# Where the normed activation and its weights lie against each other in the on-chip memory: a ramp of 32, 48, 64 bytes in place of 0, 16, 32, 48, 64

## What is computed

```
h = _rmsnorm(x, norm_pre_w[l])
proj = jnp.einsum('bsd,de->bse', h, w_in[l])
(q, k, v, o_g, z_a, i_pre, f_pre, u_b, z_b, g_a, g_b) = _partition(proj)
...
br_a = jnp.einsum('bsc,cd->bsd', y_a, w_proj_mlstm[l])
br_b = jnp.einsum('bsc,cd->bsd', y_b, w_proj_pool[l])
merged = jax.nn.sigmoid(g_a) * br_a + jax.nn.sigmoid(g_b) * br_b
out = jnp.einsum('bsd,de->bse', merged, w_out[l])
x = x + _rmsnorm(out, norm_post_w[l])
```

## Time and profile before

| | us |
|---|---|
| median of 3 runs | 1459.64 (1459.16 to 1460.74) |
| the profiled execution | 1462.16 |
| its span, first to last instruction | 1460.5 |
| TensorE busy | 1435.6 (98%) |
| VectorE busy | 850.6 (58%) |
| ScalarE busy | 707.5 (48%) |
| granted TensorE clock, mean | 0.995 |

### The profile page before, as it was taken

One profiled execution on the slowest core, in us unless ns is written; L12 is line 12 of the kernel. 1 busy time (PEld: TensorE's weight loads), 2 busy tenths in 40 slices (PEclk: granted clock), 3 DMA queues, 4 the chain that ended last, 5 costly groups with the idle time before them and its releaser, 6 DMA issues.

```text
span 1460.5 us, 27819 instructions
## 1 busy us (share of the span) xinstructions
PE 1435.6 (98%) x10878; PEld 1370.6 (94%) x10878; DVE 850.6 (58%) x1054; ACT 707.5 (48%) x929; POOL 63.1 (4%) x95
## 2 busy tenths in 40 slices
PE   6999999999999999999999999999999999999997
PEld 6999998899999999999999999888999999999786
DVE  5676674546655666545454545556555545667754
ACT  5545544545555444434344444446433346667543
POOL 0000000001110000000000000001000002111000
PEclk8999999999999999999999999999999999999999
DMA  6655645655555555555655556656555553334553
GB/s 228 201 190 184 201 166 192 196 178 177 168 175 193 175 186 190 174 194 182 199 189 191 193 190 214 247 173 217 203 172 169 178 174 121 121 121 136 208 198 122
DMA packets 71940, 266.01 MB, mean 182 GB/s; under 512 B 8088, under 2 KB 8096, under 8 KB 70944
## 3 DMA queue, kind: packets, MB, share of 16 engines
q1 hardware_dynamic: 69840, 253.12, 51.9%
q0 software_dynamic: 1440, 10.63, 2.1%
q10 hardware_dynamic: 576, 1.05, 0.2%
HBM read 260.56 MB, written 4.20 MB: 181 GB/s over the span
## 4 chain that ended last, share of the span: by engine, by line
PE 93%; DVE 3%; ACT 1%; DVEq 1%; issue 1%; DMA 0%; ACTq 0%; POOL 0%; SPq 0%; POOLq 0%
PE ps L350 23%; PE ps L354 22%; PE ps L352 22%; PE ps L342 6%; PE ps L343 6%; PE ps L344 6%; PE ps L462 2%; DVE wl L1220 1%; DVEq L1215 1%; PE ps L748 1%; PE ps L540 1%; PE ps L551 1%; DMA xn<-in_x 0%; PE ps L589 0%; ACT wh L900 0%
## 5 line engine op out<-in xcount | busy, mean ns | idle before, releaser
L1220 DVE TENSOR_TENSOR wl<-raw,wh 128x1024 fp32r<-128x1024 f32 x474 | 580.0, 1227 | 501.1 <-ACT wh L900 492.6
L900 ACT ACTIVATE wh<-raw 128x1024 fp32r<-128x1024 f32 x474 | 499.9, 1060 | 555.9 <-PE ps L354 426.7
L350 PE MATMUL ps<-xh,wh 128*128 128x256 f32 x1792 | 499.7, 279 | 3.0 <-DVE xl L1229 1.8
L352 PE MATMUL ps<-xl,wh 128*128 128x256 f32 x1792 | 498.0, 278 | 0.0
L354 PE MATMUL ps<-xh,wl 128*128 128x256 f32 x1792 | 497.9, 278 | 0.0
L350 PEld LDWEIGHTS ps<-xh,wh 128*128 128x128 f32 x1792 | 337.9, 189 | 3.7 <-DVE xl L1229 2.2
L352 PEld LDWEIGHTS ps<-xl,wh 128*128 128x128 f32 x1792 | 338.1, 189 | 0.1
L354 PEld LDWEIGHTS ps<-xh,wl 128*128 128x128 f32 x1792 | 338.0, 189 | 0.0
L350 PE MATMUL ps<-x2h,wh 128*128 128x256 f32 (+1 forms) x688 | 199.2, 290 | 1.0 <-DVE avt L1387 0.4
L354 PE MATMUL ps<-x2h,wl 128*128 128x256 f32 (+1 forms) x688 | 194.8, 283 | 0.0
L352 PE MATMUL ps<-x2l,wh 128*128 128x256 f32 (+1 forms) x688 | 194.5, 283 | 0.0
(11 more groups left out here) (337 smaller groups left out, 1772.8 us busy)
## 6 DMA issues: line engine op xcount, KB each, us to landing
raw<-in_w_stream SPq DMA_DIRECT2D x474, 512.0 KB, 3.3
xn<-in_x SPq DMA_DIRECT2D x4, 512.0 KB, 7.7
xr<-in_x POOLq DMA_DIRECT2D x1, 2048.0 KB, 12.3
x_kept<-xr POOLq DMA_DIRECT2D x1, 2048.0 KB, 9.1
x1r<-x_kept POOLq DMA_DIRECT2D x1, 2048.0 KB, 10.0
mrow<-bound_rows POOLq DMA_DIRECT2D x8, 128.0 KB, 3.5
poolw<-in_pool_w POOLq DMA_DIRECT2D x1, 1024.0 KB, 6.3
postw<-in_post_w POOLq DMA_DIRECT2D x1, 1024.0 KB, 5.2
```

Source lines behind the costliest of these rows:

```text
L350: pe.matmul(out_at(j), whr[:, c, f], hi(kc)[:, tokens], start=st, stop=False, skip_group_check=True)
L352: pe.matmul(out_at(j), whr[:, c, f], lo(kc)[:, tokens], start=False, stop=False, skip_group_check=True)
L900: act.activation(slot_view(wh_at[r], layout), raw[r][:, :, :], ACT.Copy).then_inc(wh_done, 1)
L1220: tt(slot_view(wl_at[r], layout), raw[r][:, :, :], slot_view(wh_at[r], layout).bitcast(F32), ALU.subtract).then_inc(split_done, 1)
```

## The change

The activation's ramp is cut to 0, 16, 32, 32, ... bytes (`SHORT`), and the by-feature weights that go with it start 224 bytes (56 elements) into their slot. The place becomes -224, that is 32, then 48, then 64 for all chunks from the third on. For `v` the weights start 32 bytes in: -32, -16, 0, 0, .... The ramps of `yh` and `zh`, and the layouts of `pa` and `pb`, stay. The same instructions are issued in the same order on every engine; only start addresses differ. Two things follow from the borders: the first six chunks of the first `v` group stand at 32, 48, 64, 64, 64, 64, and the first six chunks of the first `wo` group, split in the layout of `ga`, at 32 in place of 0. The 48 small matmuls of the gates (L519 to L521) read the activation at its new addresses too.

```diff
 RAMP = [4 * min(kc, 4) for kc in range(KC + 1)]
+SHORT = [4 * min(kc, 2) for kc in range(KC + 1)]
 BY_FEATURE, BY_TOKEN, SECOND, SECOND_KEYS = (48, 512), (0, 512), (0, 528), (16, 528)
-ON_RAMP, TOKEN_RAMP = (0, 512), (16, 512)
-LAYOUT_OF = {"qk": ON_RAMP, "o": ON_RAMP, "z": ON_RAMP, "u": ON_RAMP, "zb": ON_RAMP, "ga": ON_RAMP, "gb": ON_RAMP, "pa": ON_RAMP, "pb": ON_RAMP,
-             "v": TOKEN_RAMP, "wo": BY_TOKEN, "uv": BY_TOKEN, "w2": BY_TOKEN, "cq": SECOND_KEYS, "ckv": SECOND_KEYS,
+ON_RAMP, ON_SHORT, TOKEN_SHORT = (0, 512), (56, 512), (8, 512)
+LAYOUT_OF = {"qk": ON_SHORT, "o": ON_SHORT, "z": ON_SHORT, "u": ON_SHORT, "zb": ON_SHORT, "ga": ON_SHORT, "gb": ON_SHORT, "pa": ON_RAMP, "pb": ON_RAMP,
+             "v": TOKEN_SHORT, "wo": BY_TOKEN, "uv": BY_TOKEN, "w2": BY_TOKEN, "cq": SECOND_KEYS, "ckv": SECOND_KEYS,
...
-    def ramped(t):
+    def ramped(t, at=RAMP):
 
-        return lambda kc: t[:, kc * S + RAMP[kc]:(kc + 1) * S + RAMP[kc]]
+        return lambda kc: t[:, kc * S + at[kc]:(kc + 1) * S + at[kc]]
...
-        X, Y, Z = (ramped(xh), ramped(xl)), (ramped(yh), ramped(yl)), (ramped(zh), ramped(zl))
+        X, Y, Z = (ramped(xh, SHORT), ramped(xl, SHORT)), (ramped(yh), ramped(yl)), (ramped(zh), ramped(zl))
...
-            high_parts(ramped(xh), b, "norm_pre", s_x_high)
+            high_parts(ramped(xh, SHORT), b, "norm_pre", s_x_high)
...
-            low_parts(ramped(xl), ramped(xh), b, "norm_pre", s_x_high, s_x_low)
+            low_parts(ramped(xl, SHORT), ramped(xh, SHORT), b, "norm_pre", s_x_high, s_x_low)
```

More of the change, by code:

```diff
@@ L518, in _ @@
             o = ps[0:GATE_W, 4, 0:S]
-            pe.matmul(o, wgh[:, kc, :], ramped(xh)(kc), start=kc == 0, stop=False)
-            pe.matmul(o, wgl[:, kc, :], ramped(xh)(kc), start=False, stop=False)
-            last = pe.matmul(o, wgh[:, kc, :], ramped(xl)(kc), start=False, stop=kc == KC - 1)
+            pe.matmul(o, wgh[:, kc, :], ramped(xh, SHORT)(kc), start=kc == 0, stop=False)
+            pe.matmul(o, wgl[:, kc, :], ramped(xh, SHORT)(kc), start=False, stop=False)
+            last = pe.matmul(o, wgh[:, kc, :], ramped(xl, SHORT)(kc), start=False, stop=kc == KC - 1)
         last.then_inc(s_gate_sums, 1)
```

## The result

| | before | changed |
|---|---|---|
| median, us | 1460.19 (4 runs, 1459.16 to 1460.89) | 1473.72 (4 runs, 1472.58 to 1475.36) |
| ratio | | 1.0088, 95% interval 1.0075 to 1.0101 |
| span of the profiled execution, us | 1460.5 | 1472.9 |

The kernel became slower by 0.9%. The prediction said 1455.7, with a range up to 1467.5: it was wrong. The time lies near the rival "the groups fall into the slow pace at 64", form (a), which gave 1475.9; the slow pace is indeed what came, but in 21 of the 27 groups and not in all.

A forecast was written before the change was run, and what follows sets the result against it. The prediction took TensorE's matmul start pace as the bound. By-feature groups 4.05 plus `v` 0.15 minus `wo` 0.23 saved 3.97 us, from 1459.64 to 1455.7; own range 1455.0 to 1456.8, wider range 1455.0 to 1467.5 (80%).

The forecast's parts named there:

- the groups fall into the slow pace at 64: Rival: by-feature groups entering at 32 keep 1.41 us a chunk, 0.60 us a slow group; chances 16%, 11%, 17% by form.
- form (a): All 27 by-feature groups slow: +16.2 us, 1475.9 with the `v` and `wo` terms; 17% for all or nearly all.
- What bounds the kernel: TensorE, busy 98% of the span: the pace at which matmuls start sets the time, neither weights nor evacuation.
- If place alone counts, the new group is the old one from its chunk 2 on.: By-feature groups: six chunks take 8.25 us instead of 8.40, 0.15 a group, 4.05 us over 27 groups.
- After a whole chunk at place 0 it doesn't matter how the group was entered: Old ramp: `z` groups, behind other matmuls, matched `qk`: chunks 1 to 3 took 4.25 against 4.24 us, chunk 4 1.36.
- The three forms: Slow groups: all 27, 1475.9 (17%); the 12 behind other matmuls, 1464.7 (16%); the 15 others, 1466.9 (11%).
- The prices: By-feature groups: a slow group costs 0.60 us net, a fast one saves 0.15 us.
- `v`: Second `v` group's six chunks take 8.22 us instead of 8.27: 0.05 a group, 0.15 us for three groups.
- `wo`: First six `wo` chunks, moved from place 0 to 32, take 1.40 instead of 1.36 us each: at most 0.23 us more.
- Splits' addresses, gate matmuls: Splits written at 224 bytes cost nothing, covered by ScalarE's and VectorE's waits; the 48 gate matmuls stay within 0.1 us.
- The first chunk pays for entering: Rival: new chunk 0 still costs about 1.44 us; 27 by-feature groups save only 2.6 us, giving 1457.1; 12%.
- Place counts for nothing: Rival: place has no effect on the matmuls' pace, time stays at 1459.6 us; 3%.

The follow-up runs named there:

- e10: Changed kernel, every address kept, first matmul of each by-feature group on the normed activation issued twice: 1471.43 us, one run.
- e2: Changed kernel with the weights at 0 and the activation at 32, 48, 64 (same places): 1477.97 us, ratio 1.0113 to the kernel before.
- e8: Kernel before, `gb` and `v` weights moved so `gb` stays at place 64 and the last three `v` groups at 0: 1463.66 us, ratio 1.0015.
- e1: Changed kernel with the full ramp 0, 16, 32, 48, 64 back, activation and weights both 32 bytes further: 1461.90 us, ratio 1.0006 to the kernel before.
- e3: Changed kernel with places 0, 32, 48, 64, the step at 16 left out, weights at 0: 1480.18 us, ratio 1.0129 to the kernel before.
- e6: Changed kernel with all 16 chunks of by-feature groups on the normed activation at place 112: 1487.07 us, ratio 1.0171 to the kernel before.
- e7: Changed kernel with places climbing 16, 32, 48, 64: 1476.07 us, ratio 1.0098 to the kernel before.
- e4: Changed kernel with no ramp, place 64 in every chunk, `v` at 0 throughout: 1471.82 us, ratio 1.0078 to the kernel before.
- e5: Changed kernel with by-feature groups on the normed activation held at place 192, `v` at 0: 1462.27 us, ratio 1.0005 to the kernel before.
- e9: Changed kernel, activation held 64 bytes in, different weight starts for the first two chunks of some groups, the rest at place 64: 1466.27 us, one run.
- e11: Changed kernel, activation held, by-feature groups at place 64, sixteen of them starting with two chunks at 0: 1456.73 us, ratio 0.9982 to the kernel before.
- e12: e11 with `pa` and `pb` also held at place 64 and no start at 0 for `ga` 2 to 4: 1453.76 us, ratio 0.9963 to the kernel before.

## Why the prediction was wrong, point by point

- **What bounds the kernel**: right. The difference lies in the pace of TensorE's matmuls; no wait took part.
- **The step that failed**: "If place alone counts, the new group is the old one from its chunk 2 on." Place alone doesn't count. The new chunk 0 has the old chunk 2's relative place but is entered otherwise, and 21 of 27 groups ended at 1.413 (e10: with a changed entry alone, 19 of the 27 change their pace; e2, e8: the pair of addresses takes part too). I had seen both paces at 64 in the earlier trace rows and named the danger, and still gave the forecast to the case in which nothing is carried in.
- **"After a whole chunk at place 0 it doesn't matter how the group was entered"**: right as far as e1 and e3 go, in each of which all 27 groups came out alike, and it meant that removing that chunk removed what made the result the same everywhere. But the chunk only makes it the same, not good: with 0, 32, 48, 64 all came out slow.
- **The three forms**: the split was none of them, so that form (a) comes within 2.2 us of the measured time is in part luck. Both kinds of entry gave both paces: of the groups behind other matmuls 11 of 12 were slow, of the 15 others 10. Nor does the pace of the group before decide: the second `qk`, behind a slow group, was fast, the third, behind a fast one, slow.
- **The prices**: right. 0.59 to 0.62 us for a slow group where the prediction had 0.60, and 0.13 to 0.14 saved in a fast one where it had 0.15. With 21 and 6 the prediction's own numbers give 21 x 0.60 - 6 x 0.15 - 0.15 + 0.23 = +11.8. The groups gave +12.4: 0.33 of it is `pb`'s, which I didn't have, and the rest are the hundredths in the prices.
- **`v`**: right, 0.05 a group. **`wo`**: right, 0.20 against 0.23; the first six chunks take 8.39 (910.34 to 918.73). In the kernel before they took 8.19:

```profile
898.21 0.40 PE L342 MATMUL ps<-wh,mh 128*128 128x512 f32 x1
...
906.40 0.39 PE L342 MATMUL ps<-wh,mh 128*128 128x512 f32 x1
```

- **`pb`, left out**: its addresses are untouched, but it is entered from `gb`, whose weights moved. Chunk 0 takes 1.41 (743.29 to 744.70) against 1.36 in the earlier trace rows, chunks 1 and 2 2.85 against 2.87, chunk 3 1.41 against 1.36: 0.08 a group. It was 0.06 in e1, e2, e3, e6, e7 and e8, 0.04 in e10, and nothing in e4, e5, e9 and e11, where `gb` had been fast with its weights at 0 or at 128. In e8 the last chunks of `gb` stand at the same addresses as before and only their pace is the slow one. That a neighbour pays for moved addresses or for a slow group ahead of it was not in the sum.
- **Splits' addresses, gate matmuls**: nothing, as said. ScalarE 707.2 against 707.5, VectorE 850.5 against 850.6.
- **"The first chunk pays for entering"**: wrong. The first chunk took 1.40 from the fourth `qk` group on, 1.41 in the third.
- **"Place counts for nothing"**, with the rule of the Trainium skill, page "SBUF — State Buffer", section "Who interferes with whom", by which TensorE has two independent read ports and waits on nobody: that place counts for nothing agrees with no run here. Held places gave 1.36, 1.41, 1.42 and 1.44 a chunk for the same matmuls (e4, e6). Whether it is the reads of the two operands that get in each other's way is not shown, and nothing here shows TensorE waiting for another engine's reads.

## What to carry to other kernels

When equal matmuls show two paces at the same addresses anywhere in the trace, suspect a state that is entered and kept, and look at what stands ahead of each group. A warm-up that looks like pure cost (here 0.24 us a group) may be what fixes the state, and its worth is the groups times the length behind it. Don't judge a place by a chunk that passes through it: hold it for a whole group, behind each kind of work that comes before it, before building on it, and profile more than one execution where the times scatter. The cheapest form found here was to hold both operands' addresses across groups, tiles and loop turns, and to spend two chunks at place 0 only where other matmuls break the sequence. That start was followed by the fast pace in all 34 groups that had it in the profiled executions of e9, e11 and e12; how often an execution falls out of it is not shown.

## What was not expected of the hardware

- The same matmuls at the same addresses run at 1.360 or at 1.413 us a chunk of twelve, and keep that for a group or for 191 chunks (e12); with one matmul more in each group's first chunk, 19 of the 27 groups changed sides, in both directions (e10).
- Moving both operands by the same 16 bytes from chunk to chunk is no cheaper than moving them against each other: 1.41 to 1.42 in `gb`, 1.37 to 1.39 in `v` (e8), where held addresses give 1.360.
- Two chunks with the weights 32 bytes in and two with them 16 bytes in, both under an activation at 64 (places 32 and 48), took the same 1.400 and 1.396 (e9), while a chunk at place 48 with the activation at 48 and the weights at 0 took 1.42.
- What it is that locks, and why place 0 leads to the fast pace and 0, 32, 48 to the slow one, no run here shows; that stays open.
